# Hybrid decoder layer on one core: projected tiles split 256 + 272, operands of the MLP 32 bytes lower, one store and one wait moved

## The reference, cut to what matters

```
h  = rms_norm(concat([meta, x]), norm_mix_g)
p  = h @ w_in                     # 2048 x (3*1024 conv columns + 3*1024 + 64 + 64 + 160 RWKV columns)
y  = concat([short_conv(p[:, :3072]), rwkv7(token_shift(p[:, 3072:]))])
h_res = concat([meta, x]) + y @ w_out
h  = rms_norm(h_res, norm_mlp_g)
h_res = h_res + square(relu(h @ w_up)) @ w_down      # 2048 x 8192 and back
out = rms_norm(h_res, final_norm_g)[16:]
```

## Time and profile before

| what | value |
|---|---|
| median of three runs | 2312.63 us |
| profiled execution | 2299.77 us |
| its span | 2297.7 us |
| granted TensorE clock | 0.999 of full speed |

### The profile page before, as it was taken

One profiled execution on the slowest core, in us unless ns is written; L12 is line 12 of the kernel. 1 busy time (PEld: TensorE's weight loads), 2 busy tenths in 40 slices (PEclk: granted clock), 3 DMA queues, 4 the chain that ended last, 5 costly groups with the idle time before them and its releaser, 6 DMA issues.

```text
span 2297.7 us, 53673 instructions
## 1 busy us (share of the span) xinstructions
PE 2275.2 (99%) x21424; PEld 2180.3 (95%) x21424; DVE 1702.4 (74%) x2742; ACT 1113.2 (48%) x2076; POOL 299.3 (13%) x342
## 2 busy tenths in 40 slices
PE   8999999999999999999999999999999999999998
PEld 8999999999999788899999999999999999999988
DVE  7568667577586765578788778788788788787656
ACT  6534444344344423345555545555555455555436
POOL 5102012012020232200100001001001001001007
PEclk9999999999999999999999999999999999999999
DMA  7343343342442653445635536537447447357434
GB/s 245 87 106 82 95 98 83 94 109 78 100 103 72 161 178 89 141 123 134 157 102 138 139 101 157 138 93 165 120 111 165 120 112 172 95 130 200 139 97 152
DMA packets 513318, 286.26 MB, mean 125 GB/s; under 512 B 84526, under 2 KB 490544, under 8 KB 512688
## 3 DMA queue, kind: packets, MB, share of 16 engines
q1 hardware_dynamic: 478512, 224.19, 35.9%
q0 software_dynamic: 24080, 56.20, 10.9%
q10 hardware_dynamic: 10496, 2.62, 0.6%
HBM read 232.47 MB, written 50.47 MB: 123 GB/s over the span
## 4 chain that ended last, share of the span: by engine, by line
PE 87%; DVE 6%; DMA 3%; POOL 1%; issue 1%; ACT 1%; SPq 0%; ACTq 0%; POOLq 0%; DVEq 0%
PE PD L2136 15%; PE PD L2131 10%; PE PW L2384 10%; PE PW L2386 10%; PE PW L2385 10%; PE PD L2385 7%; PE PD L2384 7%; PE PD L2386 7%; PE PD L2350 1%; DVE w_lo L1530 1%; PE PD L2160 1%; PE PW L2160 1%; POOL acc L964 1%; DMA w_raw<-in_w_in 1%; POOL psq L962 1%
## 5 line engine op out<-in xcount | busy, mean ns | idle before, releaser
L2136 PE MATMUL PD<-act_both,w_hi 128*128 128x264 f32 (+1 forms) x2496 | 413.1, 287 | 0.0
L2136 PEld LDWEIGHTS PD<-act_both,w_hi 128*128 128x128 f32 x2496 | 341.6, 188 | 12.0 <-issue 6.7
L2385 PE MATMUL PW<-uf,w_hi 128*128 128x256 f32 x1120 | 312.7, 279 | 0.0
L2386 PE MATMUL PW<-uf,w_lo 128*128 128x256 f32 x1120 | 312.6, 279 | 0.0
L2384 PE MATMUL PW<-uf,w_hi 128*128 128x256 f32 x1120 | 312.6, 279 | 0.0
L1483 DVE TENSOR_TENSOR w_lo<-w_sum,w_hi 128x512 fp32r<-128x512 f32 x352 | 241.6, 688 | 67.3 <-ACT w_hi L1015 66.2
L1530 DVE TENSOR_TENSOR w_lo<-w_raw,w_hi 128x512 fp32r<-128x512 f32 x268 | 200.9, 776 | 101.2 <-ACT w_hi L1031 98.2
L1015 ACT CAST w_hi<-w_sum 128x512 fp32r<-128x512 f32 x352 | 217.7, 619 | 110.7 <-PE PW L2386 87.0
L1031 ACT CAST w_hi<-w_raw 128x512 fp32r<-128x512 f32 x268 | 159.2, 619 | 214.6 <-DMA w_raw<-in_w_in 99.9
L2136 PE MATMUL PD<-act_both,w_lo 128*128 128x264 f32 (+1 forms) x1248 | 250.8, 282 | 0.0
L2384 PE MATMUL PD<-plain,w_hi 128*128 128x256 f32 x768 | 214.5, 279 | 0.0
(11 more groups left out here) (414 smaller groups left out, 5848.4 us busy)
## 6 DMA issues: line engine op xcount, KB each, us to landing
w_raw<-in_w_in SPq DMA_DIRECT2D x200, 256.0 KB, 3.2
w_raw<-in_w_down SPq DMA_DIRECT2D x136, 256.0 KB, 2.9
w_more<-in_w_down SPq DMA_DIRECT2D x136, 256.0 KB, 2.9
w_raw<-in_w_up SPq DMA_DIRECT2D x128, 256.0 KB, 3.1
w_more<-in_w_up SPq DMA_DIRECT2D x128, 256.0 KB, 3.5
residual<-form POOLq DMA_DIRECT2D x56, 512.0 KB, 7.3
w_raw<-in_w_out SPq DMA_DIRECT2D x64, 256.0 KB, 2.9
residual<-res POOLq DMA_DIRECT2D x4, 2048.0 KB, 10.3
```

The lines of the kernel that those rows point to most:

```text
L2136: ins = M(PD[:, 2 * (n % 2) + a, cols], w, v[:, k, start:start + cols.stop - cols.start], start=begin, stop=end)
L2385: M(bank, whi, lo, start=False, stop=False, skip_group_check=True)
L2386: return M(bank, wlo, hi, start=False, stop=end, skip_group_check=True)
```

## The change: what it does

Four edits:

1. Projected tiles of 528 columns are computed as 256 columns (the last 256 of one bank) and 272 (the first 272 of the next). `pd`, `beside` and the new `half_of` hold this; `take_shifted` reads and writes such a tile as one run of 528.
2. `before_forms` shrinks from 72 to 64 columns, and `eps_t` becomes the last two columns of `par`. `uf0` to `plain3` and all that lies behind `ident` move 32 bytes down. The operands of the MLP's matmuls and `u_hi`, `u_lo` then start at multiples of 64 bytes; a few others (`keep`, `zr`, `zk`, `zv`, `cx`, `cu`, `nt0`, `rs_diag`) go from a multiple of 64 to 32 past one.
3. GpSimd stores tiles 0 to 11 of `res` as soon as it has left the loop over 14 tiles of `squares`, and tiles 12 to 15 at the end; both stores stood at the end, eight tiles each.
4. Ahead of the last down product PE waits only for `gathered` up to the second count of the last unit; it waits for all of it behind the first of the 16 tiles.

```
-    sb("before_forms", [P, 72], on=over_act)
+    sb("before_forms", [P, 64], on=over_act)
-    par = sb("par", [P, PAR_COLS])
+    par = sb("par", [P, PAR_COLS + 2])
+    eps_t = par[:, PAR_COLS:PAR_COLS + 2]
-    eps_t = sb("eps_t", [P, 2])
+WIDE = (256, 272)
     def pd(n):
-        return PD[:, 2 * (n % 2):2 * (n % 2) + 2, 0:HALF]
+        return PD[:, 2 * (n % 2):2 * (n % 2) + 2, :].rearrange("p a n -> p (a n)")[:, 512 - WIDE[0]:512 + WIDE[1]]
+    def half_of(cut, a):
+        widths, start = (WIDTHS, CUT) if cut else (WIDE, 0)
+        return (slice(512 - widths[0], 512), slice(0, widths[1]))[a], start + widths[0] * a
...
-            with pool.Fori(0, KT // 2 - 1) as i:
+            with pool.Fori(0, STORED_EARLY // 2 + 1) as i:     # STORED_EARLY = 12: seven rounds in both
                 tile(0, i)
                 tile(1, i)
+            pool.dma_start(res_view[:, 0:STORED_EARLY, :], res[:, 0:STORED_EARLY, :]).then_inc(delta_added[0], 16)
             tile(0, KT // 2 - 1)
...
-        for h in range(2):
-            cols = slice(h * KT // 2, (h + 1) * KT // 2)
-            pool.dma_start(res_view[:, cols, :], res[:, cols, :]).then_inc(delta_added[h], 16)
+        pool.dma_start(res_view[:, STORED_EARLY:KT, :], res[:, STORED_EARLY:KT, :]).then_inc(delta_added[1], 16)
...
-            nc.scalar.copy(halves(shifted[0:rows_, 1:T + 1]), src[0:rows_])
-            nc.scalar.activation(halves(keep[0:rows_, :]), src[0:rows_], ACT.Copy, scale=mun).then_inc(evacuated[n % 2], 1)
+            nc.scalar.copy(shifted[0:rows_, 1:T + 1], src[0:rows_])
+            nc.scalar.activation(keep[0:rows_, :], src[0:rows_], ACT.Copy, scale=mun).then_inc(evacuated[n % 2], 1)
...
-                            cols = (slice(512 - WIDTHS[0], 512), slice(0, WIDTHS[1]))[a] if t in cut else slice(0, HALF)
-                            start = (CUT, CUT + WIDTHS[0])[a] if t in cut else a * HALF
+                            cols, start = half_of(t in cut, a)
...
-        pe.wait_ge(gathered, GATHERED_0 + N_GATHERED * HALF_UT * FFG)
+        pe.wait_ge(gathered, GATHERED_0 + N_GATHERED * (HALF_UT * FFG - 1) + 2)
...
-        for _ in dense(KT, KQ, Q_LAST, T_LAST, u_hi, u_lo, operand=operand, one_bank=range(KT), slots=slots):
-            pass
+        for step_, _ in enumerate(dense(KT, KQ, Q_LAST, T_LAST, u_hi, u_lo, operand=operand, one_bank=range(KT), slots=slots), 1):
+            if step_ == KQ:
+                pe.wait_ge(gathered, GATHERED_0 + N_GATHERED * HALF_UT * FFG)
```

More of the change, by code:

```diff
@@ L238 @@
 SUM_AT, SCALE_AT = KT + 4, (KT + 6, KT + 7, KT + 8, KT + 9)
+STORED_EARLY = 12
 N_CONST = 4 + 6 + 4 + 4 + 3 + 4 + 2
@@ L491, in beside @@
     def beside(n):
[L493 to L496, removed]
+        bank = (PD, PD, PW, PW)[n][:, 2 * (n % 2):2 * (n % 2) + 2, :]
+        widths = WIDTHS if n in FIRST_CUT else WIDE
+        return bank.rearrange("p a n -> p (a n)")[:, 512 - widths[0]:512 + widths[1]]
+    def half_of(cut, a):
+        widths, start = (WIDTHS, CUT) if cut else (WIDE, 0)
+        return (slice(512 - widths[0], 512), slice(0, widths[1]))[a], start + widths[0] * a
     def pd_seq(n):
@@ L2157, in _ @@
                     for h in range(2):
-                        cols = (slice(512 - WIDTHS[0], 512), slice(0, WIDTHS[1]))[h] if t in FIRST_CUT else slice(0, HALF)
-                        start = (CUT, CUT + WIDTHS[0])[h] if t in FIRST_CUT else h * HALF
+                        cols, start = half_of(t in FIRST_CUT, h)
                         ins = M(bank[:, h, cols], w, v[:, k, start:start + cols.stop - cols.start], start=begin, stop=end)
```

## The result

The changed kernel takes 2328.47 us (median of 5 runs, 2327.43 to 2330.83); the kernel before, on the same chip, 2311.72 (median of 5, 2299.37 to 2313.81). The ratio is 1.0095, with a 95% interval of 1.0065 to 1.0125: slower, where 2296.8 and faster were forecast, and outside the range of 2292 to 2311. The profiled execution is 2329.04 us long with a span of 2327.0, against 2299.77 and 2297.7 before: +29.3 us of span.

The account below looks back on a forecast made before the run. PE, busy 2275.2 of 2297.7 us, was taken as the bound. Terms -2.1 - 1.1 - 11.3 - 0.4 - 0.9 = -15.8 us took 2312.63 to 2296.8 us, own range 2293 to 2300, with the fixed cost 2292 to 2311.

Parts of the forecast that it names:

- The addresses (edit 2): MLP: operands at multiples of 64 bytes make each 256-column matmul 1.08 ns cheaper; -11.3 us, between 0 and -22.6.
- exact double: MLP against last stage: 2 x 116.66 ns gives 233.3, so the cost past a multiple of 64 is proportional to columns.
- the reference of 231.16: Matmuls of 512 columns of act_both, at multiples of 64 bytes: 231.16 ns each, taken as the cost without the address penalty.
- The term of 0 by lines of 16 bytes: MLP addresses: by the skill's SBUF lines of 16 bytes, operands start no better than before, so the gain is 0.
- The same edit in the last stage: Last down product: 192 matmuls of 512 columns each 2.14 ns cheaper at multiples of 64 bytes; -0.4 us.
- The store (edit 3): Early MLP: storing twelve tiles early removes PE's wait of 2.12 us; -2.1 us, between 0 and -2.1.
- The wait (edit 4): Step from MLP to last down product: PE starts sooner by not awaiting DVE's last adds; -1.1 us, between 0 and -1.1.
- The halves (edit 1): Projected tiles in two halves: 816 couples each 1.1 ns cheaper; -0.9 us, between -2.2 and +0.8.
- The tail: GpSimd's last 27 tiles: DVE's shifted adds could slow them, +9.7 us; with the first rival 2319.1 us, slower; chance 0.05.
- The first rival: MLP: fixed cost of 2.2 ns per matmul, start of 256 columns irrelevant, no MLP gain; -3.2 us, 2309.4 us; chance 0.30.
- the 12.86 us: Whole kernel: the median lies 12.86 us above the profiled execution, and this gap was kept for the forecast.

Follow-up runs that it names:

- weights_up: Kernel before with 32 bytes of padding ahead of the weights, moving them up while the operands in act_both's space stay: 2324.52 us, ratio 1.0082.
- The small program: Stand-alone matmuls in the MLP's order with operands and weights at chosen bytes, computing nothing of the layer; 256 columns at distance 0 took 120.0 ns, at 112 113.3.
- addresses_only: Kernel before with the operands 32 bytes lower and nothing else: 2333.8 us, ratio 1.0134.
- widths_only: Kernel before with the 256 and 272 column widths, their half_of and read-out, and nothing else: ratio 0.9985, span 2298.8 us.
- rest_only: Changed kernel with the operands put back where they were; widths, early store and later wait stay: 2295.69 us, ratio 0.9976 to the kernel before.
- the first small program: Stand-alone stretches of 36 matmuls varying columns, operand and weight bytes, steps and PSUM column: 256 columns took 120.0 ns at +0, 116.7 at +32.
- bench_places, bench_distances, bench_fine: One of the stand-alone matmul programs with chosen operand and weight bytes; the text does not say which, so no separate time is given.
- distance_112: rest_only with every moving operand of MLP and last stage 112 bytes behind the weights, matrix of ones moved: 2261.10 us, ratio 0.9819 to the kernel before.
- store_only: Kernel before with the store of 12 tiles early and nothing else: ratio 1.0006.

## Why the prediction was wrong

- **The addresses (edit 2), the term of the MLP.** This step failed. The prediction took 231.16 and 233.30 ns as the two sides of one thing, a start at a multiple of 64 bytes, and carried half of the 2.14 ns over to 256 columns: -11.3 us, with 0 and -22.6 as its ends. Measured: +3.34 ns a matmul, +34.9 us, 120.0 ns where 115.58 was forecast. Three things were wrong in it. The place alone is not what counts, but its distance from the weights: `weights_up` makes `plain` slow without moving it. The move took this distance from 32 to 0. 256 columns do not follow 512: at distance 0, 512 columns are at their fastest (226.7) and 256 slow (120.0); at 32, 512 cost 233.3 and 256 only 116.7. The "exact double" that spoke for a proportional cost was chance: it holds at 32 and not at 0 or 64. And the reference of 231.16 was none: the rows of `act_both` are 2112 bytes apart, 64 modulo 256, so its reads go through four distances and 231.2 is a mixture of them. The small program takes 226.7, 228.9, 233.3 and 233.3 ns at the distances 0, 64, 128 and 192 alone, and 231.2 and 231.1 in two stretches with the rows of `act_both`, at its byte and 64 further on. What could have been seen in the profile: the two stretches differed in their row step too, a second difference beside the one that the term was built on. No row excluded a loss, yet this term ended at nothing, though the prediction itself said that no row shows 256 columns alone at a multiple of 64; for the halves it did put bounds on both sides of zero (-2.2 and +0.8). The term of 0 by lines of 16 bytes, which the prediction set beside its own, is not borne out either: of the distances 96 and 112, both multiples of 16, one takes 120.0 ns and the other 113.3.
- **The same edit in the last stage.** -0.4 forecast, -1.25 measured (44.90 to 43.55 us, less the 0.1 that is the wait's; `addresses_only` has 43.68). Right in sign, three times larger, by the same mis-taken reference: the 192 matmuls are at 226.8 ns, not 231.2. The sign is in part luck, since the rule that gave it is the one that failed.
- **The store (edit 3).** -2.1 forecast. The wait of 2.12 us is gone, the 3072 KB landed by 954, and what is next is PE's own work, as the prediction had it.
- **The wait (edit 4).** -1.1 forecast. The step from one stage to the other goes from 1.12 to 0.12 us, and the first matmul behind it from 0.34 to 0.24: -1.1.
- **The halves (edit 1).** The couple is at 240.0 ns as forecast, from 241.1; the MLP starts 0.69 us sooner, of -0.9. `widths_only`, whose MLP starts 0.74 us later, can neither confirm nor deny so small a sum. The distance replaces the rule that the 1.1 ns were worked out by, so the 240.0 agrees for a reason that is not shown, and may be luck.
- **The tail.** It neither gained nor lost (64.50 and 64.51 us). The rival that had a loss there, the only one forecast slower (2319.1 us), came nearest in its time by a mechanism that did not happen. No rival had a loss in the MLP.
- **The first rival** (fixed cost, MLP unchanged, 2309.4) was nearer than the forecast, and not right. The Trainium skill, "TensorE: Matmul & The Clock Gate", section "Wait — 56ns, not 53.3ns?", states the columns over 2.4 GHz and about 2.5 ns more, and speaks of no addresses. By it 256 columns would take an estimated 109.2 ns and 512 215.8; the prediction had tested the 2.5 ns alone, against half of the 231.16 that is a mixture. Here 256 columns (106.7 ns) cost 6.7 to 15.6 ns more by distance and entry and 512 (213.3) 13.3 to 23.3, so for these float32r matmuls with a weight load each the trace does not agree.
- **The sum without the failed term**: -2.1 - 1.1 - 0.4 - 0.9 = -4.5 us; `rest_only`, which lacks the 0.4 and so had -4.1 to bring, is 3.8 us shorter in span and 5.3 in its median.

What stays open is why a distance has the cycle it has. The runs show the dependence, and a period of 256 bytes at the distances 0 and 32; which port or buffer of the chip makes it was not tried. With 240 columns and fewer (192, 128) the first small program shows about 111.7 ns whatever the width, so the weight load may be the other party, with about that length; this is an inference, not shown.

## What to carry to other kernels

Where PE never waits, the cadence of its matmuls is the time, and it can depend on the byte distance between moving operand and weights: measure it with a small program over all distances before placing operands, in the kernel's own widths and product order, since no arithmetic on two stretches gives it. When two stretches are compared to price an address, list all in which they differ (row step, weights' place, width) first. For a property that no row shows alone, a loss belongs in the range as much as a gain.

## What the runs showed of the hardware

- With 256 columns a float32r matmul costs 113.3 to 122.2 ns start to start with nothing changed but the distance between its operands modulo 256 and the matmuls ahead of it, at a granted clock of 1.00; with 512 columns 226.7 to 236.7 (`bench_places`, `bench_distances`, `bench_fine`). In the whole kernel, distance 112 gives 113.3 ns, 32 116.7 and 0 and 96 120.0.
- A pace can have two values at one distance (192: 117.8 and 113.3 in the small program). In the kernel before it is the likely reason why its times lie in two groups, 2298 to 2306 and 2310 to 2314 us. `store_only`'s profiled execution is of the upper group (2308.97 us; others of its runs take 2297 to 2299), and its window reads

```profile
1100.00:2100.00 1000.00, 1000.00 (x8493) 1000.00 (x8492) 808.05 (x1341) 531.16 (x1052) 59.69 (x50) 1.00 0.52 130
```

  that is 117.8 ns with the beat 119, 116, 118, where the profiled executions of the lower group have 116.7: 10,464 x 1.1 = 11.5 us. No profile of the kernel before from its upper group exists. That these are the 12.86 us by which the median of before lay above its profiled execution is likely, and was carried over unexplained in the prediction. The five runs of `distance_112` lie within 1 us.
- Idle time of PE early in the MLP varies from 1.84 to 2.73 us between the profiled executions of six kernels without the early store, so an edit of 1 to 2 us is told by its own rows of a timeline and not by a ratio.
